# A chunked recurrence on one core: inverse levels as 32x32 products, a block last level, and a state sum on TensorE

## The chip, the cores and the metric

The kernel runs on one core of a Trainium2 chip, as one launch. The metric is the device time in microseconds (us), the median over runs. All products here are float32. In the profile such a product appears as two records (two weight loads and two matmuls), so "record" below means one of those two.

## The reference, cut to what matters

The program is a two-layer block network (layer 0: an RWKV-7 mixer and a SwiGLU; layer 1: a pooling mixer and a mixture of experts) followed by an attention layer. The change touches only the recurrence of the RWKV-7 mixer, which runs for 16 heads of width 64, in two directions, over 256 context and then 512 latent positions:

```python
def wkv7_scan(s0, r, w, kk, a, k, v):
    def step(s, inp):
        r_t, w_t, kk_t, a_t, k_t, v_t = inp
        s_kk = jnp.einsum('bhvk,bhk->bhv', s, kk_t)
        s = (s * w_t[:, :, None, :] - s_kk[..., None] * (kk_t * a_t)[:, :, None, :]
             + v_t[..., None] * k_t[:, :, None, :])
        return s, jnp.einsum('bhvk,bhk->bhv', s, r_t)
```

## The kernel before, in words

The function `pairs` does not step over positions. It cuts the 768 positions into 12 chunks of 64 (`CH`), numbered n; n = 0 to 3 are the context, n = 4 to 11 the latent part. Within a chunk the recurrence is a triangular system, and the kernel needs the inverse of a 64x64 triangular matrix. It works on 8 pairs of heads, p = 0 to 7. One head of the pair lies in partitions 0 to 63, the other in 64 to 127 (`heads`), and both directions (d = 0, 1) stand side by side in the columns. So each step handles four 64x64 matrices.

For each chunk the steps are, by their names in the plan:

- `score n` (L1168): products that give the matrix and the key products, masked by VectorE into `LK` (L1434). GpSimd adds the diagonal (`I`, L1056) and masks the first transposed inverse (`firstT`, L1059).
- `trans n` (L1184): PE transposes of the chunk's inputs by the identity, copied by ScalarE into `TR` (L1346).
- `first n` (L1438): VectorE's transpose of the first inverse.
- `X lev.n` and `T lev.n` for lev = 0 to 4: one doubling level of the inverse. X (L1192) is matrix times inverse, 4 products of 64x64; VectorE multiplies it by the level's mask into `Xs` (L1444). T (L1204) multiplies by the transposed inverse, again 4 products; ScalarE copies the new inverse into `TB` (L1350). VectorE's `turn lev.n` (L1441) transposes it for the next level.
- `akv n` (L1215, L1218), then the chain over chunks: `U n` (L1227, L1230; copy L1358), `Z n` (the state; L1237, L1239) and, for latent chunks, `Y n` (the output; L1252 to L1256, copy L1367). VectorE makes the new state from `Z n` in two steps: L1450 adds the old state to the product into `Z_sum`, L1455 multiplies by the decay into `Z`. `U n+1` waits for it.

The order is written out once as a list, `plan`, and every engine walks through it, each executing its own entries in order; semaphores (`Marks`) tie them together. Four chunks make a quad. `quad(g)` interleaves the front of quad g (score, trans, first, X, T, turn) with the chain of quad g-1: after each block of four X or four T entries one link of the chain stands (`U n`, or `Y n` and `Z n`), for the first eight blocks. `score` of the next quad waits until ScalarE has copied the last level of the chunk that held the same PSUM bank (L1350 from T4). The inputs of pair p+1 (`feature`: L1073 and L1099 on the PE; sigmoids, scans and reciprocals elsewhere) and the normalised outputs of pair p-1 (`output`) are spread over the quads by their place in the list. After the last pair one quad of chain alone remains. Input loads and masks are issued by SyncE's queue (L926 to L943).

Of the kernel before, what the change touches and what calls it, by code (L numbers as in the profile page):

```python
# [21 lines left out]
P = 128  # L22
# [403 lines left out]
class Kernel:  # L426
# [347 lines left out]
    def pairs(self, TW, TA, TG, YG, xr, s_wr):  # L774
# [5 lines left out]
        NG, LAST, H6, MASKS = N * QUADS, 4, TOK // 2, 12  # L780
        FRONT = ("score", "trans", "first", "X", "T", "turn")
# [24 lines left out]
        def quad(g):  # L806
# [61 lines left out]
        pe_f = self.marks("front_pe", [x for x in fronts if x.rstrip("0123456789.") in ("score", "trans", "X", "T")])  # L868
        pe_c = self.marks("chain_pe", links)
        act_f = self.marks("front_act", following(fronts, {"trans": ["tr"], "T": ["t"]}))  # L870
        act_c = self.marks("chain_act", following(links, {"akv": ["akv"], "U": ["U"], "Y": ["Y"]}))
        dve_f = self.marks("front_dve", following(fronts, {"score": ["LK"], "first": ["first"], "X": ["x"], "turn": ["turn"]}))
        dve_c = self.marks("chain_dve", [y for x in links if x[0] == "Z" for y in ([f"sum{x[1:]}"] if x != "Z0" else []) + [f"z{x[1:]}"]])
# [10 lines left out]
        with ExitStack() as st:  # L884
# [7 lines left out]
            Zb, Zs, Us = self.sb(st, "Z", 2, 2, CH), self.sb(st, "Z_sum", 2, CH), self.sb(st, "Us", 2, CH)  # L892
            mC, mL, mT = self.sb(st, "mask_score", 2, 4, CH), self.sb(st, "mask_level", 6, 2, CH), self.sb(st, "mask_turned", 2, CH)
            RB = self.sb(st, "r_rows", 4, SEQ)
            id2, scan = self.sb(st, "id_twice", CH), self.sb(st, "scan_steps", TOK)
            TB, AT, Xs = self.sb(st, "tb", 2, 4, 2, 2, CH), self.sb(st, "at", 4, 2, 2, CH), self.sb(st, "xs", 4, 2, CH)
# [3 lines left out]
            heads = (slice(0, CH), slice(CH, P))  # L900
            pair0 = COLS["pair"][0]
# [16 lines left out]
            with nc.Block() as block:  # L918
                @block.sync
                def _(sp):  # L920
# [17 lines left out]
                    for hh in heads:  # L938
# [3 lines left out]
                        sp.dma_start(mL[hh, :, :, :].rearrange("p l d n -> p (l d) n"), block("mL", hh, 12)).then_inc(s_mask, 16)  # L942
                        sp.dma_start(id2[hh, :], A["consts"][hh, hh]).then_inc(s_mask, 16)  # L943
                    r_load(0)
# [11 lines left out]
                def _(pool):  # L956
# [80 lines left out]
                    for kind, p, x in plan:  # L1037
# [13 lines left out]
                        if head == "score":  # L1051
                            if p == 0 and n == 0:
                                pool.wait_ge(s_diag, 2)
# [9 lines left out]
                def _(pe):  # L1063
# [56 lines left out]
                    for kind, p, x in plan:  # L1120
# [30 lines left out]

                        if head == "score":
# [32 lines left out]
                        elif head == "X":  # L1185
                            if lev:
# [3 lines left out]
                            for d in range(2):  # L1190
                                for hh in heads:
                                    last = pe.matmul(ps[hh, i, d * CH:(d + 1) * CH], M[hh, d, 0, :], tb[hh, d, 0, :],  # L1192
                                                     start=True, stop=True)
                        elif head == "T":
# [5 lines left out]
                            for d in range(2):  # L1200
                                to = 256 + d * CH
# [58 lines left out]
                def _(act):  # L1260
# [64 lines left out]
                    for kind, p, x in plan:  # L1325
# [22 lines left out]
                        elif head == "T":  # L1348
                            act.wait_ge(pe_f.sem, pe_f.at(x, p))
                            S.activation(TB[:, s, i, :, int(lev == LAST), :], ps[:, i, 256:384].rearrange("p (d n) -> p d n", d=2),  # L1350
# [20 lines left out]
                def _(dve):  # L1371
# [37 lines left out]
                    for kind, p, x in plan:  # L1409
# [13 lines left out]
                        if head == "score" and p == 0 and n == 0:  # L1423
                            dve.wait_ge(s_mask, MASKS * 16)
                            V.tensor_tensor(mL[:, :, :, :].rearrange("p l d n -> p (l d) n"), mL[:, :, :, :].rearrange("p l d n -> p (l d) n"),
                                            id2[:, :].unsqueeze(1).broadcast_to([P, 12, CH]), ALU.add).then_inc(s_diag, 1)
                            dve.wait_ge(s_diag, 1)
                            for d in range(2):
                                last = V.tensor_copy(mT[:, d, :], mL[:, 0, 1 - d, :])
                            last.then_inc(s_diag, 1)  # L1430
# [8 lines left out]
                        elif head == "turn":  # L1439
                            dve.wait_ge(act_f.sem, act_f.at(f"t{lev}.{n}", p))  # L1440
                            V.transpose(TB[:, s, i, :, 1, :], TB[:, s, i, :, 0, :]).then_inc(*dve_f.did(x))  # L1441
                        elif head == "X":
                            dve.wait_ge(pe_f.sem, pe_f.at(x, p))
                            V.tensor_tensor(Xs[:, i], ps[:, i, 0:P].rearrange("p (d n) -> p d n", d=2), mL[:, lev + 1, :, :],  # L1444
                                            ALU.mult).then_inc(*dve_f.did("x" + x[1:]))
                        elif head == "Z":
                            dve.wait_ge(pe_c.sem, pe_c.at(x, p))
                            b = ps[:, 5, 3 * P:4 * P].rearrange("p (d n) -> p d n", d=2)
                            if n:
# [1657 lines left out]
```

## Time and profile before

| what | value |
|---|---|
| median of 3 runs | 3277.22 us (3274.03 to 3282.49) |
| profiled execution, its own time | 3275.92 us |
| its span, first to last instruction | 3274.3 us |
| mean granted TensorE clock | 0.946 of full |
| PE, PEld busy | 2868.9 us, 2351.9 us |
| DVE, ACT, POOL busy | 1926.9 us, 1388.2 us, 536.5 us |

The recurrence runs from about 341 to 1132 us of the span. PE is TensorE's matmul, PEld its weight load, DVE VectorE, ACT ScalarE, POOL GpSimd, SPq SyncE's DMA issues. Matmuls are pipelined: a record lasts much longer than the distance to the next one's start, so the cost of one more record is read from distances of starts.

### The profile page before, as it was taken

Reading aid. Unit: us, or ns where it says so; the run is one execution under the profiler, and the core shown is the slowest. Engines: PE = TensorE matmul, PEld = TensorE weight load, DVE = VectorE, ACT = ScalarE, POOL = GpSimd, SP = SyncE. Lnnn points to the kernel's source line nnn. Section 1 sums busy time; section 2 is a strip of 40 time slices with the busy share of each in tenths; the row PEclk is TensorE's granted clock in tenths of the full one; section 3 lists DMA queues with packets and bytes.
Section 4 is the critical chain, followed back from the end, with each engine's and each line's share of the span. In section 5 each row is a group of like instructions: output and inputs, shape, how many; then the busy total and the mean of one; then the engine's idle time right before and its main releaser. Section 6 shows DMA issues by size and latency. Waiting matters only on the chain. (4 is left out here: it accounts for less than half of the span.)

```text
span 3274.3 us, 70012 instructions
## 1 busy us (share of the span) xinstructions
PE 2868.9 (88%) x30245; PEld 2351.9 (72%) x30245; DVE 1926.9 (59%) x3058; ACT 1388.2 (42%) x2040; POOL 536.5 (16%) x489
## 2 busy tenths in 40 slices
PE   7998798998989589999834999999976987779999
PEld 2564687787878467887614999999973754558877
DVE  5431455666565445765673888888876146456652
ACT  2002445445445333212223777777764335443331
POOL 3001445453344110000001000000010025200000
PEclk9999999999999789999966999999997989889999
DMA  5643000000000146664305999999962210122222
GB/s 194 221 154 103 7 20 20 20 21 20 10 14 4 64 152 242 264 266 162 124 13 227 372 370 364 369 366 365 371 256 68 94 52 26 52 80 102 90 101 79
DMA packets 74015, 483.10 MB, mean 148 GB/s; under 512 B 11123, under 2 KB 13043, under 8 KB 32288
## 3 DMA queue, kind: packets, MB, share of 16 engines
q1 hardware_dynamic: 59360, 418.48, 34.2%
q0 software_dynamic: 12096, 52.43, 4.4%
q10 hardware_dynamic: 2304, 8.39, 0.6%
q8 instruction: 208, 3.41, 0.4%
q14 instruction: 47, 0.39, 0.0%
HBM read 457.73 MB, written 34.13 MB: 150 GB/s over the span
## 5 line engine op out<-in xcount | busy, mean ns | idle before, releaser
L2267 DVE TENSOR_TENSOR sb_moe_w_lo<-w_ring,sb_moe_w_hi 128x1408 fp32r<-128x1408 f32 (+1 forms) x132 | 255.3, 1935 | 68.2 <-ACT sb_moe_w_hi L2221 67.3
L2167 PE MATMUL ps<-sb_moe_w_hi,sb_x_feat_lo 128*128 128x352 f32 x832 | 274.1, 329 | 11.5 <-DVE sb_moe_w_lo L2267 11.5
L2169 PE MATMUL ps<-sb_moe_w_hi,sb_x_feat_hi 128*128 128x352 f32 x832 | 268.4, 323 | 0.0
L2168 PE MATMUL ps<-sb_moe_w_lo,sb_x_feat_hi 128*128 128x352 f32 x832 | 267.6, 322 | 0.0
L2221 ACT ACTIVATE sb_moe_w_hi<-w_ring 128x2816 fp32r<-128x2816 f32 x80 | 204.4, 2556 | 0.2
L2167 PEld LDWEIGHTS ps<-sb_moe_w_hi,sb_x_feat_lo 128*128 128x128 f32 x832 | 156.8, 188 | 17.4 <-issue 17.0
L2167 PE MATMUL ps<-sb_moe_w_hi,sb_hid_feat_lo 128*128 128x256 f32 x572 | 163.2, 285 | 3.9 <-DVE sb_hid_feat_lo L2293 3.9
L2169 PE MATMUL ps<-sb_moe_w_hi,sb_hid_feat_hi 128*128 128x256 f32 x572 | 161.8, 283 | 0.0
L2168 PE MATMUL ps<-sb_moe_w_lo,sb_hid_feat_hi 128*128 128x256 f32 x572 | 161.8, 283 | 0.0
L1441 DVE STREAM_TRANSPOSE sb_tb<-sb_tb 128x128 f32<-128x128 f32 x384 | 106.0, 299 | 90.9 <-ACT sb_tb L1350 88.6
L2168 PEld LDWEIGHTS ps<-sb_moe_w_lo,sb_x_feat_hi 128*128 128x128 f32 x832 | 157.6, 189 | 0.0
L2169 PEld LDWEIGHTS ps<-sb_moe_w_hi,sb_x_feat_hi 128*128 128x128 f32 x832 | 156.7, 188 | 0.0
L1192 PEld LDWEIGHTS ps<-sb_tb,w_ring 64*64 64x64 f32 x3840 | 127.3, 135 | 38.5 <-issue 20.8
L1192 PE MATMUL ps<-sb_tb,w_ring 64*64 64x64 f32 x3840 | 145.4, 220 | 9.6 <-ACT sb_tb L1350 7.4
L233 PE MATMUL ps<-sb_ffn_features,sb_hi_ffn 128*128 128x512 f32 x352 | 141.2, 401 | 10.7 <-DVE sb_ffn_features L372 8.1
L233 PE MATMUL ps<-sb_conv_hl,sb_hi_conv 128*128 128x512 f32 x352 | 140.4, 399 | 10.2 <-DVE sb_conv_hl L372 10.2
L1434 DVE TENSOR_TENSOR w_ring<-ps,sb_mask_score 128x512 f32<-128x512 f32 (+1 forms) x96 | 57.8, 603 | 149.0 <-PE ps L1168 149.0
L1350 ACT ACTIVATE sb_tb<-ps 128x128 f32<-128x128 f32 x480 | 117.6, 279 | 63.3 <-PE ps L1204 59.8
L235 PE MATMUL ps<-sb_conv_hh,sb_hi_conv 128*128 128x512 f32 x352 | 140.6, 399 | 0.0
L234 PE MATMUL ps<-sb_conv_hh,sb_lo_conv 128*128 128x512 f32 x352 | 138.8, 394 | 0.0
L235 PE MATMUL ps<-sb_ffn_features,sb_hi_ffn 128*128 128x512 f32 x352 | 138.8, 394 | 0.0
L234 PE MATMUL ps<-sb_ffn_features,sb_lo_ffn 128*128 128x512 f32 x352 | 138.7, 394 | 0.0
(518 smaller groups left out, 7939.1 us busy)
## 6 DMA issues: line engine op xcount, KB each, us to landing
w_ring<-w_moe_up SPq DMA_DIRECT2D x67, 1408.0 KB, 8.4
sb_hm<-w_ada SPq DMA_DIRECT2D x48, 1024.0 KB, 6.9
w_ring<-w_ffn SPq DMA_DIRECT2D x22, 1024.0 KB, 4.8
w_ring<-w_up SPq DMA_DIRECT2D x22, 1024.0 KB, 4.9
sb_t_again<-w_moe_up SPq DMA_DIRECT2D x13, 1408.0 KB, 8.4
sb_hm<-w_moe_up SPq DMA_DIRECT2D x13, 1408.0 KB, 8.2
sb_b_again<-w_moe_up SPq DMA_DIRECT2D x13, 1408.0 KB, 7.6
w_ring<-w_moe_down SPq DMA_DIRECT2D x13, 1408.0 KB, 7.5
```

The costliest lines, as they stand in the source:

```text
L233: pe.matmul(out, w_hi[:, at:at + P], lo(k), start=(k == 0), stop=False)
L234: pe.matmul(out, w_lo[:, at:at + P], hi(k), start=False, stop=False)
L235: last = pe.matmul(out, w_hi[:, at:at + P], hi(k), start=False, stop=(k == KT - 1))
L1192: last = pe.matmul(ps[hh, i, d * CH:(d + 1) * CH], M[hh, d, 0, :], tb[hh, d, 0, :], start=True, stop=True)
L1350: S.activation(TB[:, s, i, :, int(lev == LAST), :], ps[:, i, 256:384].rearrange("p (d n) -> p d n", d=2), ACT.Copy).then_inc(*act_f.did("t ...
L1434: V.tensor_tensor(LK[:, s, i, :, ::by, :], ps[:, i, :].rearrange("p (d o n) -> p d o n", d=2, o=4)[:, :, ::by, :], mC[:, :, ::by, :], ALU. ...
L1441: V.transpose(TB[:, s, i, :, 1, :], TB[:, s, i, :, 0, :]).then_inc(*dve_f.did(x))
L2167: pe.matmul(out, x_lo, w_hi, start=first, stop=False)
L2168: pe.matmul(out, x_hi, w_lo, start=False, stop=False)
L2169: return pe.matmul(out, x_hi, w_hi, start=False, stop=end)
L2221: S.activation(WH[:, s, :], raw[r], ACT.Copy).then_inc(rounded[s], 1)
L2267: return V.tensor_tensor(WL[:, s, w], raw[raw_at(c, i)[0]][:, w], WH[:, s, w].bitcast(F32), ALU.subtract)
```

## The change

It has four parts.

1. Levels 0 to 3 (inverses of blocks up to 32 wide) no longer multiply whole 64x64 matrices but only their diagonal 32x32 blocks. Each head has two of them, so four 32-partition groups (`subs`) work side by side: X and T are each 8 products of 32x32 where there were 4 of 64x64. What VectorE masks, ScalarE copies and VectorE turns is 64 columns wide instead of 128. T of level 3 is written back to full width by VectorE (`wide3`, masked by `own_half`) instead of by ScalarE.
2. The last level is one 32x32 block off the diagonal per matrix: X4 is 4 products, T4 is 4, and a new entry `S4` (at the end of the quad) is 4 more; ScalarE copies after S4, and `score` of the next quad waits for that copy.
3. The old state is added in PSUM: `Z n` for n > 0 has 4 more 64x64 products with the identity, and VectorE's L1450 goes.
4. The level masks are loaded per 32-partition group: 22 mask DMAs instead of 12, and a few set-up instructions on VectorE.

```diff
-        NG, LAST, H6, MASKS = N * QUADS, 4, TOK // 2, 12
-        FRONT = ("score", "trans", "first", "X", "T", "turn")
+        NG, LAST, H6, MASKS, SUB = N * QUADS, 4, TOK // 2, 22, 32
+        FRONT = ("score", "trans", "first", "X", "T", "S", "turn")
...
+            out += [(p, f"S{LAST}.{n}") for n in cur]
...
+                    for g in subs:
+                        sp.dma_start(mL[g, :, :, :].rearrange("p l d n -> p (l d) n"),
+                                     block("mL", g, 2 * LAST + 2)[:, 2:2 * LAST + 2, :]).then_inc(s_mask, 16)
+                        sp.dma_start(id1[g, :], A["consts"][g, g]).then_inc(s_mask, 16)
...
+                        def across(d, g):
+                            own, to = subs[g], 256 + d * SUB
+                            pe.matmul(ps[subs[g ^ 1], i, to:to + SUB], x2[own, 0, :], tb[own, d, 1, homes[g]], start=True, stop=True)
+                            return pe.matmul(ps[own, i, to:to + SUB], tb[own, d, 0, homes[g]], ident[own, own], start=True, stop=True)
...
-                                for hh in heads:
-                                    last = pe.matmul(ps[hh, i, d * CH:(d + 1) * CH], M[hh, d, 0, :], tb[hh, d, 0, :],
-                                                     start=True, stop=True)
+                                for g in range(4):
+                                    cols = low if 0 < lev < LAST else homes[g]
+                                    if lev < LAST:
+                                        last = pe.matmul(ps[subs[g], i, d * SUB:(d + 1) * SUB], M[subs[g], d, 0, homes[g]],
+                                                         tb[subs[g], d, 0, cols], start=True, stop=True)
+                                    elif g % 2 == d:
+                                        last = pe.matmul(ps[subs[g ^ 1], i, 0:SUB], M[subs[g], d, 0, homes[g ^ 1]],
+                                                         tb[subs[g], d, 0, cols], start=True, stop=True)
...
-                                for hh in heads:
-                                    w, src = (tb[hh, d, 1, :], x2[hh, d, :]) if lev < LAST else (x2[hh, d, :], tb[hh, d, 1, :])
-                                    last = pe.matmul(ps[hh, i, to:to + CH], w, src, start=True, stop=True)
+                                for g in range(4):
+                                    own, cols = subs[g], low if 0 < lev < LAST else homes[g]
+                                    if lev < LAST:
+                                        last = pe.matmul(ps[own, i, to:to + SUB], tb[own, d, 1, cols], x2[own, d, :], start=True, stop=True)
+                                    elif d == 0 and g % 2:
+                                        last = across(d, g)
+                        elif head == "S":
+                            pe.wait_ge(pe_f.sem, pe_f.at("T" + x[1:], p))
+                            for g in (0, 2):
+                                last = across(1, g)
...
+                                if n:
+                                    for hh in heads:
+                                        pe.matmul(ps[hh, 5, to:to + CH], ident[hh, hh], Zb[hh, n % 2, d, :], start=False, stop=False)
...
+                        elif head == "T" and lev == LAST - 1:
+                            dve.wait_ge(pe_f.sem, pe_f.at(x, p))
+                            both, to = ps[:, i, 256:256 + CH], own_half[:, 0:2]
...
-                                V.tensor_tensor(Zs[:, :, :], b, Zb[:, n % 2, :, :], ALU.add).then_inc(*dve_c.did(f"sum{n}"))
```

## Rows read from the trace of the kernel before

**Rows 1.** The page: granted TensorE clock in 40 slices of the span.
```profile
PEclk9999999999999789999966999999997989889999
```
**Rows 2.** Busy time by stretch: start:end, length, each engine (xinstructions), clock, DMA.
```profile
341.00:380.00 39.00, 32.16 (x656) 25.38 (x658) 17.32 (x54) 15.55 (x34) 18.94 (x18) 0.87 0.01 2
380.00:1095.00 715.00, 648.45 (x18540) 584.33 (x18538) 432.89 (x1299) 348.38 (x954) 315.61 (x290) 1.00 0.05 15
1095.00:1132.00 37.00, 17.97 (x282) 13.10 (x278) 5.83 (x11) 6.40 (x18) 5.05 (x4) 0.64 0.00 1
```
**Rows 3.** Groups by line and shape: busy us, mean ns | idle before, and its releaser.
```profile
L1192 PE MATMUL ps<-sb_tb,w_ring 64*64 64x64 f32 x3840 | 145.4, 220 | 9.6 <-ACT sb_tb L1350 7.4 <-DVE sb_tb L1438 1.3
L1350 ACT ACTIVATE sb_tb<-ps 128x128 f32<-128x128 f32 x480 | 117.6, 279 | 63.3 <-PE ps L1204 59.8
L1204 PE MATMUL ps<-sb_xs,sb_tb 64*64 64x64 f32 x3072 | 114.7, 221 | 4.3 <-DVE sb_xs L1444 4.2
L1444 DVE TENSOR_TENSOR sb_xs<-ps,sb_mask_level 128x128 f32<-128x128 f32 x480 | 114.5, 272 | 26.4 <-PE ps L1192 26.4
L1441 DVE STREAM_TRANSPOSE sb_tb<-sb_tb 128x128 f32<-128x128 f32 x384 | 106.0, 299 | 90.9 <-ACT sb_tb L1350 88.6
...
L1346 ACT ACTIVATE w_ring<-ps 128x512 f32<-128x512 f32 x96 | 57.3, 597 | 66.5 <-PE ps L1184 66.5
...
L1434 DVE TENSOR_TENSOR w_ring<-ps,sb_mask_score 128x512 f32<-128x512 f32 x64 | 44.2, 691 | 83.7 <-PE ps L1168 83.7
...
L1450 DVE TENSOR_TENSOR sb_Z_sum<-ps,sb_Z 128x128 f32<-128x128 f32 x80 | 22.4, 280 | 51.6 <-PE ps L1239 51.5
```
**Rows 4.** PE in order of time, saturated: start us, us to the end, line, xrecords.
```profile
602.05 0.40 PE L1218 MATMUL ps<-sb_tb,w_ring 64*64 64x64 f32 x8
602.28 0.28 PE L1184 MATMUL ps<-sb_consts,sb_ex 64*64 64x64 f32 x4
```
**Rows 5.** PEld in order of time: weight loads of 128 columns for 2-column matmuls.
```profile
166.45 1.64 PEld L631 LDWEIGHTS ps<-sb_consts,sb_xx 128*128 128x128 f32 x14
```
**Rows 6.** Two lines' weight loads: duration ns min/median/max, first and last start, forms.
```profile
L631 PEld LDWEIGHTS ps<-sb_consts,sb_xx x64: 190/192/192, 166.1 to 237.0; 128*128 128x128 f32 x64
...
L2470 PEld LDWEIGHTS ps<-sb_hm,sb_head_sums x32: 106/110/110, 2617.0 to 2631.1; 128*32 128x32 f32 x32
```
**Rows 7.** PE and PEld in order of time, products 32 columns wide.
```profile
2616.96 1.92 PE L2470 MATMUL ps<-sb_hm,sb_head_sums 128*32 128x512 f32 x16
2618.81 0.50 PE L2453 MATMUL ps<-sb_lo_qkv,sb_qkv_hh 128*128 128x512 f32 x1
2616.96 0.16 PEld L2470 LDWEIGHTS ps<-sb_hm,sb_head_sums 128*32 128x32 f32 x8 [0.37 <-issue]
```
**Rows 8.** PE in order of time around feature products between X products.
```profile
637.44 0.68 PE L1192 MATMUL ps<-sb_tb,w_ring 64*64 64x64 f32 x16
638.05 1.56 PE L1073 MATMUL ps<-sb_tw,sb_w_pair 128*128 128x384 f32 x4
```
**Rows 9.** Waits inside the recurrence: engine line <- releaser, us in total, times, longest.
```profile
PE ps L1227 <- DVE sb_Z L1455: 35.7, 32, 2.7
PE ps L1073 <- ACT sb_sg L1275: 15.4, 8, 2.4
```
**Rows 10.** All engines in order of time, around one wait for the state.
```profile
586.11 1.10 PE L1192 MATMUL ps<-sb_tb,w_ring 64*64 64x64 f32 x32
586.68 0.91 DVE L1389 RECIPROCAL sb_kk<-sb_kk 128x128 f32<-128x128 f32 x1
587.51 0.23 DVE L1450 TENSOR_TENSOR sb_Z_sum<-ps,sb_Z 128x128 f32<-128x128 f32 x1
587.78 0.29 DVE L1455 TENSOR_TENSOR sb_Z<-sb_Z_sum,sb_pend 128x128 f32<-128x128 f32 x1
588.21 0.33 PE L1227 MATMUL ps<-sb_at,sb_tb 64*64 64x64 f32 x4 [1.00 <-DVE sb_Z L1455]
```
**Rows 11.** SyncE's queue: the last of the mask DMAs.
```profile
292.98 0.65 SPq L943 DMA_DIRECT2D sb_id_twice<-consts  x1
```

More of the change, by code:

```diff
@@ L866, in following @@
             return [y + x[len(x.rstrip("0123456789.")):] for x in names for y in table.get(x.rstrip("0123456789."), ())]
-        pe_f = self.marks("front_pe", [x for x in fronts if x.rstrip("0123456789.") in ("score", "trans", "X", "T")])
+        pe_f = self.marks("front_pe", [x for x in fronts if x.rstrip("0123456789.") in ("score", "trans", "X", "T", "S")])
         pe_c = self.marks("chain_pe", links)
-        act_f = self.marks("front_act", following(fronts, {"trans": ["tr"], "T": ["t"]}))
+        act_f = self.marks("front_act", following([x for x in fronts if not x.startswith((f"T{LAST - 1}.", f"T{LAST}."))],
+                                                    {"trans": ["tr"], "T": ["t"], "S": ["t"]}))
         act_c = self.marks("chain_act", following(links, {"akv": ["akv"], "U": ["U"], "Y": ["Y"]}))
-        dve_f = self.marks("front_dve", following(fronts, {"score": ["LK"], "first": ["first"], "X": ["x"], "turn": ["turn"]}))
-        dve_c = self.marks("chain_dve", [y for x in links if x[0] == "Z" for y in ([f"sum{x[1:]}"] if x != "Z0" else []) + [f"z{x[1:]}"]])
+        dve_f = self.marks("front_dve", [x for x in following(fronts, {"score": ["LK"], "first": ["first"], "X": ["x"], "turn": ["turn"],
+                                                               "T": ["wide"]})
+                                         if not x.startswith("wide") or x.startswith(f"wide{LAST - 1}.")])
+        dve_c = self.marks("chain_dve", [f"z{x[1:]}" for x in links if x[0] == "Z"])
         pool_f = self.marks("front_pool", following(fronts, {"score": ["I", "firstT"]}))
@@ L900, in pairs @@
             heads = (slice(0, CH), slice(CH, P))
+            subs = [slice(g * SUB, (g + 1) * SUB) for g in range(4)]
+            low, high = slice(0, SUB), slice(SUB, CH)
+            homes = (low, high, low, high)
             pair0 = COLS["pair"][0]
@@ L941, in _ @@
                                 sp.dma_start(mC[hh, d, o:o + 2, :], block("mK", hh, 4)[:, 2 * d:2 * d + 2, :]).then_inc(s_mask, 16)
[L942 removed]
+                        for d in range(2):
+                            sp.dma_start(mT[hh, d, :], block("mL", hh, 2)[:, 1 - d, :]).then_inc(s_mask, 16)
                         sp.dma_start(id2[hh, :], A["consts"][hh, hh]).then_inc(s_mask, 16)
+                    for g in subs:
+                        sp.dma_start(mL[g, :, :, :].rearrange("p l d n -> p (l d) n"),
+                                     block("mL", g, 2 * LAST + 2)[:, 2:2 * LAST + 2, :]).then_inc(s_mask, 16)
+                        sp.dma_start(id1[g, :], A["consts"][g, g]).then_inc(s_mask, 16)
                     r_load(0)
@@ L1185, in _ @@
                         elif head == "X":
-                            if lev:
+                            if lev == LAST:
+                                pe.wait_ge(dve_f.sem, dve_f.at(f"wide{lev - 1}.{n}", p))
+                            elif lev:
                                 pe.wait_ge(act_f.sem, act_f.at(f"t{lev - 1}.{n}", p))
@@ L1424, in _ @@
                             dve.wait_ge(s_mask, MASKS * 16)
+                            V.tensor_tensor(mT[:, :, :], mT[:, :, :], id2[:, :].unsqueeze(1).broadcast_to([P, 2, CH]),
+                                            ALU.add).then_inc(s_diag, 1)
                             V.tensor_tensor(mL[:, :, :, :].rearrange("p l d n -> p (l d) n"), mL[:, :, :, :].rearrange("p l d n -> p (l d) n"),
[L1426 to L1430, printed above, removed]
+                                            id1[:, :].unsqueeze(1).broadcast_to([P, 2 * LAST, SUB]), ALU.add).then_inc(s_diag, 1)
+                            for g in range(4):
+                                V.memset(own_half[subs[g], g % 2:g % 2 + 1], 1.0).then_inc(s_diag, 1)
+                                V.memset(own_half[subs[g], 1 - g % 2:2 - g % 2], 0.0).then_inc(s_diag, 1)
+                            dve.wait_ge(s_diag, 10)
                         if head == "score":
@@ L1439, in _ @@
                         elif head == "turn":
-                            dve.wait_ge(act_f.sem, act_f.at(f"t{lev}.{n}", p))
-                            V.transpose(TB[:, s, i, :, 1, :], TB[:, s, i, :, 0, :]).then_inc(*dve_f.did(x))
+                            cols = low
+                            if lev == LAST - 1:
+                                dve.wait_ge(dve_f.sem, dve_f.at(f"wide{lev}.{n}", p))
+                                cols = slice(0, CH)
+                            else:
+                                dve.wait_ge(act_f.sem, act_f.at(f"t{lev}.{n}", p))
```

41 lines of the change are left out of this document (25 added, 16 removed).

## The prediction

> **What bounds the kernel now.** I read the page first: the span is 3274.3 us and the TensorE clock is nearly always full [rows 1]. The chain that ended last lies wholly behind the recurrence, so it says nothing about the stage that is changed. The busy times by stretch do [rows 2]: in 380 to 1095 us TensorE is busy 648.5 of 715 us at clock 1.00, VectorE 432.9, ScalarE 348.4, GpSimd 315.6. So the recurrence is bound by TensorE with some 10% of waits in it. The next stage begins only when this block has ended, so what the recurrence saves comes off the end one for one.
>
> The groups by line [rows 3] say what TensorE does there: X (L1192) has 3840 records, T (L1204) as many, 3072 in the row shown and 768 of the last level. Their mean of 220 ns is not their cost, for they overlap. The cost is read in order of time [rows 4]: eight 64x64 records take 602.05 to 602.28; over many such pairs of rows it is 0.233 us, so 29.2 ns per record. The waits [rows 9] are led by U for the new state, 35.7 us in 32 times, and the second feature product for ScalarE's sigmoid, 15.4 us in 8.
>
> **Part 1, inverse as 32x32.** Per chunk X and T are now 5 levels x 2 x 4 products x 2 records = 80 records; over 96 chunks 7680 x 29.2 ns = 224.3 us. Changed, levels 0 to 3 are 4 x 2 x 8 x 2 = 128 records, X4, T4 and S4 8 each, 152 in all: 14,592 over 96 chunks. Everything hangs on what one costs.
>
> Two products of 64x64 on the two heads run together: a round of two records takes 58.3 ns. A single-file series of 128-column weight loads [rows 5] takes 1.64 us for fourteen, the last one's length counted in; less its 0.19 us [rows 6] that is 13 distances of 0.112 us. 58.3 and 112 ns lie on one line: 0.83 ns per weight column plus 5 ns. For 32 columns it gives 31.7 ns per round. How many records share a round? In [rows 7] four products, 32 columns wide with 512 moving ones, stand side by side: 16 records go by in 1.86 us, 0.116 us each, where 512 moving columns at the same 0.83 ns are 0.43 us; so four tiles do work at once. A record would then cost 31.7 / 4 = 7.9 ns.
>
> The bounds: from below, the eight weight loads of [rows 7] take 0.16 us with the last one's 0.11 us [rows 6] in it, so they start 7 ns apart, which is the fastest supply of records that I see: 6.7 ns x 14,592 = 98 us. From above, no row shows records at a lasting pace under 29.2 ns: 426 us. I take 7.9 ns: 115.3 us, a change of -109.0 us, for both the sharing and the weight line are in rows; but that TensorE is fed a pair of instructions every 8 ns for long stretches is in no row.
>
> Here a page speaks against the change. The row shows records starting 7 ns apart in a burst of eight. The Trainium skill (TensorE: Matmul & The Clock Gate, "Back-to-back issue gap"; TensorEngine Tiling, "Instruction Overhead") says that a matmul of fewer than about 60 columns costs as much as one of 60, about 25 ns from start to start. If that holds for each record, X, T and S cost 14,592 x 25 ns = 365 us, 141 us more than now; if it holds per tile, a round of 31.7 ns is above it and nothing changes. The burst speaks for the second, and proves it only for a burst. By the Trainium skill's 25 ns per record the kernel would take 3276 + 141 + 50 = 3467 us.
>
> **Changes of tile shape.** Feature products (128x128) between X products [rows 8]: sixteen records from 637.44 should be over at 637.91, the next form starts at 638.05. So 0.10 to 0.14 us are lost, and the other way it is similar: the four feature records take until 639.54, 1.49 us, where 4 x 0.323 = 1.29 are due. The next form's first record starts 0.07 us before the modelled end of the last one (637.44 + 0.68), and 0.20 us of the 1.49 are lost over two changes and a weight load of 128 columns. Walking through the plan, TensorE now changes form 130 times; with X, T and S at 32x32 between score, akv, trans, U, Y, Z at 64x64 it is 527 times. 397 more x 0.10 us = +39.7 us; bounds 0 (no loss between these two forms, which the trace doesn't have) and 0.17 us each, 67 us. The Trainium skill (TensorEngine Tiling, "Key Properties") has the rule that a change of tiling mode drains the engine; the trace agrees for the forms it has.
>
> **Part 2, the last level.** Before, X4 and T4 of a quad take 2 x 0.93 us, and each covers the other's hand-over. Hand-over times: a matmul ends 0.22 us after its start at 64 columns, so (less 32 x 0.83 ns) about 0.19 at 32; then about 0.06 us to the next engine, an estimate between 0.04 and 0.14, the distances behind L1450 and L1455 in [rows 10]; then VectorE or ScalarE. These cost 0.27 and 0.28 us at 128 columns; from 512 columns (0.69, 0.60) the slope is 1.1 and 0.8 ns per column, so 0.20 and 0.23 us at 64 [rows 3]. After, X4 is 4 x 8 x 7.9 = 0.25 us long, but T4.0 can start only 0.06 + 0.19 + 0.06 + 0.17 + 0.06 = 0.54 us after X4.0: 0.29 us idle. S4 is 0.25 us long, but the next quad's score waits for the copy behind S4.0, 0.06 + 0.19 + 0.06 + 0.23 + 0.06 = 0.60: 0.35 us. 24 quads x 0.64 = +15.4 us. In levels 0 to 3 the hand-over of about 0.6 us lies under a block of 0.51 us and the link behind it (0.47 to 1.4 us), but for the first quad and the odd late wait: +3 us. If no link covered it, it would cost 0.1 us per block, 192 blocks, 19 us.
>
> **Part 3, the state.** Ten of the twelve chunks of a pair get 4 products more: 80 x 8 x 29.2 ns = +18.7 us; both bounds are near, for it is the form of [rows 4]. L1450 goes from between Z and U. Where U waits [rows 9], X ends issuing at 587.05 and U starts at 588.21: VectorE had a reciprocal of 0.91 us in hand, then sum and scale. After: T's block is 0.42 us shorter and so is X's, the sum's 0.28 us are gone, identity and changes of form add 0.4; U is ready some 0.3 us earlier and the state some 0.7 us earlier. What is late next is the reciprocal, which stays. So of 35.7 us [rows 9] I take 8 off; bounds 0 and -20. In the last quad, which is chain alone, sum and identity weigh the same: 0.
>
> **The rest.** The feature product waits for a sigmoid that starts behind U's copy, a fixed time, so less TensorE work before it lengthens the wait by 0.2 us, 8 times: +1.6 us. VectorE's and ScalarE's shorter operations are off the path, hidden by TensorE's work: 0; were they the bound, it would be a gain. Level 3's copy moves to VectorE, 0.28 us at full width, in a stretch where it has 40% to spare. Mask loads: ten more DMAs at 0.65 us on SyncE's queue [rows 11] end at about 303 us, the masks are wanted at 344; behind them stand only the loads for r and pair 1, with tens of us of slack: 0. Without that slack it would be 6.5 us.
>
> **Sum.** -109.0 + 39.7 + 15.4 + 3.0 + 18.7 - 8.0 + 1.6 = -38.6 us. Against the profiled execution's own 3275.9 us that is 3237; it lies 1.3 us under the median of the runs, so 3238. The break-even is close: with the other terms as they are, the change pays only while a 32x32 record costs less than (224.3 - 70.4) / 14,592 = 10.5 ns.
>
> **Rivals.**
> *TensorE can't take small records that fast.* The supply of instructions, two per record, becomes the bound of each X and T block. For it: the trace has 14.6 ns per instruction as its best lasting pace. Against it: the bursts, and that the 64-column pace is explained by weight columns alone. It turns the sign from 10.5 ns per record. At 14.6 ns, half of today's distance, X, T and S cost 213 us (-11.3), the short-block stalls vanish, and with 39.7 + 18.7 - 8.0 the kernel takes 3316. At 29.2 ns, it is 3277 + 252 = 3529. I take 3316 as this rival's time. Chance 0.27.
> *Saved time comes back as waits.* Blocks of 0.5 us no longer cover the hand-over through VectorE and ScalarE, whose queues also hold reciprocals of 0.9 us. For it: [rows 9, 10], U already waits behind them. Against it: VectorE is busy only 61% of the stretch and its own work shrinks. If each of the 192 blocks in levels 0 to 3 idles 0.2 us more, it eats the 38 us: 3277. Chance 0.13.
> *No loss between 64x64 and 32x32.* Then -78 us: 3199. For it: the trace shows the loss only against forms with 128 rows. Against it: the loss stands on both sides of the feature products. Chance 0.10.
> *The clock falls.* Four 32x32 tiles work with a quarter of the array, two of 64x64 with half, and fewer records stand in a block. In 1095 to 1132 us, with TensorE busy under half, the granted clock averaged 0.64, between the levels of 1.2 and 2.4 GHz [rows 2]. If a quarter of the recurrence ran at the low level: 0.25 x 650 = 160 us more, about 3400. Against it: busy shares near 90% hold 1.00. Chance 0.05.
>
> **How the numbers follow.** My forecast, 3238, has 0.45. What a measurement of this kernel can tell from no change is 0.3%, 10 us. Faster: forecast, free change of form and a third of the waits rival, 0.59. Same: the rest of that rival, 0.09. Slower: the first rival and the clock, 0.32. The range for 8 in 10 reaches from the free change of form, 3195, to just past the first rival's 3316: 3325. The forecast's own range is 3215 to 3262.
>
> **What would show it.** Eight X products of a chunk (16 records) should follow one another in 0.13 us instead of the 0.23 us of eight records; by the first rival in 0.23 us or more. At each U, Y, Z between X and T a gap of 0.10 us or more. TensorE's busy time in the recurrence should fall by some 60 us. Between X4 and T4, and between S4 and score, idle of about 0.3 us each. The wait of U for the state should be below 35.7 us. I am wrong if X's records stand 12 ns or more apart, or if VectorE becomes the releaser of most T blocks.

## The result: 3.6% slower, and the profile after

The changed kernel takes 3392.95 us (3389.14 to 3398.11, 4 runs); the kernel before, beside it, 3275.62. The ratio is 1.036 (1.034 to 1.038): 117 us slower, where 39 us faster was forecast and 3325 us was the end of the range.

The page after, its span, the clock in 40 slices, and the packets, MB and time of the queue that brings instructions (before: 70012 instructions in a span of 3274.3 us, 208 packets; the clock in [rows 1]):

```profile
span 3392.8 us, 85054 instructions
PEclk8999898888988869999986799999997998889999
q8 instruction: 267, 4.37, 0.5%
```

Slices 4 to 14, counted from 0, are the recurrence, and only there does the clock differ much from [rows 1]. The busy times by stretch, for [rows 2]:

```profile
341.00:380.00 39.00, 30.04 (x900) 22.87 (x902) 15.59 (x57) 12.70 (x29) 20.00 (x18) 0.81 0.01 3
380.00:1100.00 720.00, 620.94 (x21935) 532.85 (x21934) 309.09 (x1123) 277.05 (x749) 284.45 (x259) 0.88 0.05 16
1100.00:1240.00 140.00, 114.32 (x4202) 101.52 (x4195) 45.91 (x195) 38.55 (x128) 30.00 (x34) 0.87 0.02 4
```

No engine is fuller than before. TensorE is busy 86% of the main stretch where it was 91%, VectorE 43% where it was 61%, and the clock is 0.88 instead of 1.00. So something keeps TensorE from its work that is none of the engines. The groups by line, for [rows 3] (L1214 is X, L1230 is T, L1389 and L1493 their copies, L1272 the identity products):

```profile
L1230 PE MATMUL ps<-sb_xs,sb_tb 32*32 32x32 f32 x6144 | 95.8, 201 | 28.6 <-issue 27.4 <-DVE sb_tb L1487 0.5 <-DVE sb_xs L1493 0.2
L1214 PE MATMUL ps<-sb_tb,w_ring 32*32 32x32 f32 x6144 | 89.6, 201 | 35.7 <-issue 31.7 <-DVE sb_tb L1479 3.4 <-ACT sb_tb L1389 0.5
L1389 ACT ACTIVATE sb_tb<-ps 128x64 f32<-128x64 f32 x384 | 69.5, 226 | 108.0 <-PE ps L1230 57.2 <-PE ps L1168 49.2
L1493 DVE TENSOR_TENSOR sb_xs<-ps,sb_mask_level 128x64 f32<-128x64 f32 x384 | 68.8, 209 | 57.7 <-PE ps L1214 55.9
L1272 PE MATMUL ps<-sb_Z,sb_consts 64*64 64x64 f32 x640 | 54.0, 245 | 1.6 <-issue 1.5
```

Read what ended the idle time before X and T: "issue", 31.7 and 27.4 us, meaning that no semaphore ended it. The list of waits, for [rows 9], shows each such stop to be long (total, times, longest):

```profile
PE ps L1214 <- issue: 31.7, 27, 3.1
PE ps L1230 <- issue: 27.4, 26, 2.7
PE ps L1086 <- ACT sb_sg L1310: 15.9, 7, 2.4
```

U's wait for the state, 35.7 us in 32 times before, has left the head of the list:

```profile
PE ps L1259 <- DVE sb_Z L1506: 1.5, 3, 0.5
```

In order of time TensorE looks like this (start, us to the end, records, idle before):

```profile
656.04 0.82 PE L1230 MATMUL ps<-sb_xs,sb_tb 32*32 32x32 f32 x64
656.79 0.33 PE L1287 MATMUL ps<-sb_FR,sb_Z 64*64 64x64 f32 x4
...
658.99 0.33 PE L1272 MATMUL ps<-sb_Z,sb_consts 64*64 64x64 f32 x4 [0.82 <-issue]
...
660.69 0.57 PE L1230 MATMUL ps<-sb_xs,sb_tb 32*32 32x32 f32 x38
662.47 0.42 PE L1230 MATMUL ps<-sb_xs,sb_tb 32*32 32x32 f32 x19 [1.22 <-issue]
```

The first line is a block of T as forecast: 64 records in 0.75 us to the next line's start, 11.7 ns each with the change of form. The last two are one block of T, broken after 38 of its 64 records by 1.22 us in which nothing is waited for (the view's window ends inside the last row; 26 records follow). I listed all stops over 0.45 us without a semaphore from 380 to 1215 us and counted TensorE's instructions between them: there are 91, 107.8 us in all, and each lies a whole multiple of 256 instructions behind the one before (256, 512, 768, give or take one). A record is two instructions, its weight load and its matmul, so the smallest distance is 128 records. Each stop ends 1.2 to 1.7 us after a 16 KB packet on the instruction queue has landed. In the kernel before there is one such stop, of 0.6 us.

To see where the 117 us lie I took TensorE's records from the recurrence's first to its last 64x64 product and split every distance between starts: array work (each record at its undisturbed pace: 29.2 ns, 7.9 ns, or the feature products' own); what the low clock level adds to it; up to 0.1 us (0.2 at the low level) at each change of form; gaps over 150 ns, with a semaphore ("waits") or without ("supply"); the rest, which is small idles. us:

```
                      before  after  difference  forecast
array work             631.7  542.0      -89.7      -90.3
low clock level          6.7   45.3      +38.6          0
changes of form         12.5   57.3      +44.8      +39.7
small idles             21.8   78.8      +57.0       }
waits on semaphores     97.2   64.2      -33.0       } +12.0
supply                   1.3  106.9     +105.6          0
length                 771.2  894.4     +123.2      -38.6
```

The two profiled spans differ by 118.5 us, so some 5 us of the 123.2 come back outside the recurrence. TensorE's busy time in it rose from 698.6 to 765.3 us, though its array work fell: changes of form and the low clock count as busy.

### The profile page after: what moved, and what is told of

Same layout as the page of the kernel before. It is cut to its first block and busy times, and to the rows that moved or that the text cites. A ratio compares the mean times of both kernels' runs of the same rounds, so it can differ in the third digit from the quotient of the medians.

```text
span 3392.8 us, 85054 instructions
## 1 busy us (share of the span) xinstructions
PE 2939.4 (87%) x37797; PEld 2387.6 (70%) x37797; DVE 1845.5 (54%) x3081; ACT 1346.8 (40%) x1944; POOL 533.2 (16%) x489
## 5 line engine op out<-in xcount | busy, mean ns | idle before, releaser
L233 PE MATMUL ps<-sb_ffn_features,sb_hi_ffn 128*128 128x512 f32 x352 | 141.2, 401 | 10.7 <-DVE sb_ffn_features L372 8.1
L1487 DVE STREAM_TRANSPOSE sb_tb<-sb_tb 128x64 f32<-128x64 f32 (+1 forms) x384 | 89.0, 249 | 102.0 <-ACT sb_tb L1389 101.2
L1713 DVE SCALAR_TENSOR_TENSOR sb_ada_acc<-sb_hm,sb_c_silu,sb_ada_acc 128x512 f32<-128x512 f32 x168 | 126.3, 752 | 10.5 <-DMA sb_hm<-w_ada 3.2
L1230 PE MATMUL ps<-sb_xs,sb_tb 32*32 32x32 f32 x6144 | 95.8, 201 | 28.6 <-issue 27.4
L1214 PE MATMUL ps<-sb_tb,w_ring 32*32 32x32 f32 x6144 | 89.6, 201 | 35.7 <-issue 31.7
```

Of the source, the lines that this page charges most:

```text
L233: pe.matmul(out, w_hi[:, at:at + P], lo(k), start=(k == 0), stop=False)
L1214: last = pe.matmul(ps[subs[g], i, d * SUB:(d + 1) * SUB], M[subs[g], d, 0, homes[g]], tb[subs[g], d, 0, cols], start=True, stop=True)
L1230: last = pe.matmul(ps[own, i, to:to + SUB], tb[own, d, 1, cols], x2[own, d, :], start=True, stop=True)
L1487: V.transpose(TB[:, s, i, :, 1, cols], TB[:, s, i, :, 0, cols]).then_inc(*dve_f.did(x))
L1713: V.scalar_tensor_tensor(out=ACC[:, j % 2, :], in0=w, scalar=scale, in1=ACC[:, j % 2, :], op0=ALU.mult, op1=ALU.add).then_inc(s_ada, 1)
```

## The experiments

The theory after the result: the instructions reach TensorE at a lasting pace of about 128 records per 3.5 us, records of 7.9 ns run through them faster, and the stops, the clock that falls with them, and the changes of form cost more than the array work saved. The rivals: the last level's uncovered hand-overs, or the new state sum, are what costs; or TensorE has a least distance per small record, wherever its instructions come from.

### Part 3 alone (e1_sum)

```diff
+                                if n:
+                                    for hh in heads:
+                                        pe.matmul(ps[hh, 5, to:to + CH], ident[hh, hh], Zb[hh, n % 2, d, :], start=False, stop=False)
...
-                                V.tensor_tensor(Zs[:, :, :], b, Zb[:, n % 2, :, :], ALU.add).then_inc(*dve_c.did(f"sum{n}"))
```

> The kernel before with part 3 alone: the old state is added by identity products on TensorE, VectorE's sum is gone. 1280 more records in the 64x64 form. Supply theory (TensorE gets its instructions in blocks of 256, no faster than one block per about 3.5 us, which is 13.7 ns per instruction; a 64x64 record already takes 14.6 ns per instruction, so this form stays just inside the supply): +18.7 us of TensorE work, less some of U's waits, 3280 to 3294, no stalls without a semaphore. Change-of-form theory (the slowdown comes from the 397 more changes between 64x64 and 32x32): the same, since no form changes here. If part 3 were the cause of the slowdown, 3340 or more.

Measured: 3257.84 us (3252.32 to 3265.81), ratio 0.994 (0.992 to 0.996): 20.7 us faster, faster than both kernels, and below what was expected. U's wait for the state falls from 35.7 us in 32 times to

```profile
PE ps L1227 <- DVE sb_Z L1454: 6.3, 15, 0.5
```

The identity products cost their 18.7 us (array work 650.3 against 631.7), and waits of all kinds fall by 40. The sum on TensorE is not what costs. But the stops without a semaphore, of which none was expected, are there: a dozen over 0.45 us, and supply rises from 1.3 to 12.9 us. So 64x64 records run into the supply too.

Why the wait fell so far is to be read from VectorE's operation that makes the new state, and from GpSimd beside it. Before (durations in ns as min/median/max, then the rows in order of time), and last the same operation in e1_sum:

```profile
L1455 DVE TENSOR_TENSOR sb_Z<-sb_Z_sum,sb_pend x80: 291/293/3161, 393.6 to 1112.5; 128x128 f32<-128x128 f32 x80
611.83 3.42 POOL L992 TENSOR_TENSOR sb_ex<-sb_ex,sb_kk 128x1536 f32<-128x1536 f32 x1
612.24 3.16 DVE L1455 TENSOR_TENSOR sb_Z<-sb_Z_sum,sb_pend 128x128 f32<-128x128 f32 x1
615.55 0.33 PE L1227 MATMUL ps<-sb_at,sb_tb 64*64 64x64 f32 x4 [1.55 <-DVE sb_Z L1455]
L1454 DVE TENSOR_TENSOR sb_Z<-ps,sb_pend x88: 226/291/293, 392.2 to 1103.7; 128x128 f32<-128x128 f32 x88
```

With the sum on VectorE, L1455 reads both its inputs from SBUF (`Z_sum` and `pend`). In 23 of 80 times it lasts 0.77 to 3.16 us instead of 0.29, and each of these ends 0.15 us after a GpSimd operation does; none of the short ones lies inside a long GpSimd operation. In e1_sum it reads PSUM and `pend`, and lasts 0.29 us at most in all 88, 33 of which lie inside a long GpSimd operation. Of U's 35.7 us, 21.6 in 17 times stood behind such a held L1455. The other 15 waits, behind the reciprocals and in the last quad, fell from 14.0 to 6.3 us.

### Everything but part 3 (e2_inverse)

The changed kernel with L1450's sum back on VectorE (the lines above the other way round).

> The changed kernel with part 3 taken back: parts 1, 2 and 4 alone. Both theories: most of the slowdown stays, 3370 to 3388, with some 90 stalls at block ends. It falls by more than the 18.7 us of identity products only if these fed the stalls: supply theory says a little more (10 blocks less at 3.5 us are 35 us at most, so 3358 at the lowest), change-of-form theory says exactly 19 us or less.

Measured: 3401.22 us, ratio 1.039 (1.036 to 1.041), above the range that both theories gave. Only 8 us are left of part 3's gain: U's wait for the state is 19.4 us here and 1.5 in the changed kernel, no more than the identity products cost. Supply costs 81 us and the low clock 56. The loss is in the inverse.

### The changed kernel with few small records (e3_few)

In X and T of levels 1 to 3 one 32x32 product is left where there are eight. This leaves out part of the inverse's work, while blocks, copies and semaphores stay.

```diff
-                                    if lev < LAST:
+                                    if lev < LAST and (lev == 0 or d + g == 0):
```

> The changed kernel, in which X and T of levels 1 to 3 issue one 32x32 product instead of eight (the other blocks of PSUM keep level 0's values, so the inverse is not computed). All waits, hand-overs, copies and all 527 changes of form stay; TensorE's records fall from 152 to 68 per chunk. Supply theory: the stalls at block ends vanish (under 10 us in all), the granted clock in the recurrence returns to 0.98 or more, and the time falls by well over the 84 x 96 x 7.9 ns = 64 us of array work, to 3200 to 3250, under the kernel before. Change-of-form theory: only the 64 us go, 3329.

Measured: 3259.43 us, ratio 0.994 (0.992 to 0.996). 8064 records fewer take away 134 us. At 7.9 ns they are 64 us of array work; supply falls from 106.9 to 18.1 (11 stops are left), the low clock from 45 to 34, and waits rise by 30. So the stops come with the number of instructions. The supply theory had expected more: under 10 us of stops, the clock at 0.98 or more and 3250 us or less. The same run says why it fell short: 172 us less array work than e1_sum (478.1 against 650.3), and the same time. Between those two stand changes of form (55.5 against 12.6), small idles (84.2 against 20.9), waits (93.7 against 57.1) and the clock (33.7 against 6.2).

### Part 2 alone, at 64x64 elsewhere (e4_last), and with part 3 (e6_last_sum)

```diff
+                                if lev == LAST:
+                                    for g in (d, d + 2):
+                                        last = pe.matmul(ps[subs[g ^ 1], i, 0:SUB], M[subs[g], d, 0, homes[g ^ 1]],
+                                                         tb[subs[g], d, 0, homes[g]], start=True, stop=True)
+                                    continue
...
+            out += [(p, f"S{LAST}.{n}") for n in cur]
```

> The kernel before with part 2 alone: levels 0 to 3 stay 64x64 products, the last level is one 32x32 block off the diagonal, with S at the end of the quad. 88 records per chunk instead of 80, of which 24 small; 48 more changes of form. By array work 96 x (467 - 190) ns = -26.6 us, +15.4 for the two uncovered hand-overs, +5 for changes of form: 3269. Supply theory: the 192 small instructions of a chunk-quad of X4, T4, S4 run ahead of the supply and wait at about one block end per quad for up to 1 us: 3272 to 3290. Change-of-form theory: 3265 to 3275.

Measured: 3324.93 us, ratio 1.015 (1.013 to 1.018): 46 us slower. U's wait for the state grew:

```profile
PE ps L1248 <- DVE sb_Z L1483: 45.1, 23, 2.7
PE ps L1159 <- DVE sb_xs L1470: 8.0, 15, 1.3
PE ps L1178 <- ACT sb_tb L1375: 4.5, 13, 1.0
```

Both theories had it well under 3300. The entries S4 lengthen the plan, and what is spread over it by place comes to stand elsewhere. Three times per pair U now waits long for the state: once 1.71 us behind a reciprocal (602.73 us), and twice, 2.7 and 2.2 us (622.37 and 635.18), behind the operation that makes the state, held while GpSimd works, as in e1_sum's rows. These held ones are 32.2 us of the 45.1. The other two rows are the last level's hand-overs. With part 3, where that operation reads PSUM, this can be told apart.

> Parts 2 and 3 without part 1: e4_last with the old state added on TensorE. In e4_last the largest wait is U for the state, 45 us, because the four S entries per quad shift the reciprocals' places in the plan onto the state's. If that is what made e4_last slow, taking VectorE's sum away removes some 25 to 30 us of it at +18.7 us of TensorE work, as it did in e1_sum: 3305 or a little less, still above the kernel before. If the uncovered hand-overs behind X4 and S4 are the cause, the waits of T4 and score stay and the time is the same 3305, with the state's wait under 15 us. If the two effects are independent, e4_last and e1_sum add up: 3278.5 + 46.4 - 20.7 = 3304.

Measured: 3278.26 us, ratio 1.000 (0.999 to 1.001), 20 us more than e1_sum, and 27 less than the 3305 expected: the two effects don't add up, for part 3 takes the held operations away. Its wait for the state:

```profile
PE ps L1248 <- DVE sb_Z L1482: 8.3, 9, 1.1
```

So part 2 beside part 3 costs 20 us. Array work is 26.5 us less than in e1_sum; waits (+13.0), supply (+12.5), the clock (+9.3), small idles (+10.7) and form (+4.8) are more.

### Parts 1, 3 and 4 with the last level at 64x64 (e8_levels)

```diff
-                                    elif g % 2 == d:
-                                        last = pe.matmul(ps[subs[g ^ 1], i, 0:SUB], M[subs[g], d, 0, homes[g ^ 1]],
-                                                         tb[subs[g], d, 0, cols], start=True, stop=True)
+                                    elif g < 2:
+                                        hh = heads[g]
+                                        last = pe.matmul(ps[hh, i, d * CH:(d + 1) * CH], M[hh, d, 0, :], tb[hh, d, 0, :],
+                                                         start=True, stop=True)
```

> Parts 1, 3 and 4 without part 2: levels 0 to 3 as 32x32 products, the last level again as four 64x64 products for X and for T, full-width mask and copy, no S. 144 records per chunk, 128 of them small. Supply theory: part 1 alone makes most of the slowdown, because its bursts of small records empty the instruction buffer: 3355 to 3385, with more than 60 stops at block ends. Last-level theory (the slowdown is the sum of what parts 1 and 2 do to the waits, and part 2 alone costs 46 us): 3393 - 46 = 3347 or less, with stops unchanged.

Measured: 3369.41 us, ratio 1.029 (1.027 to 1.031), 112 us more than e1_sum. With part 2's 20 us that makes 132 of the 135 us that lie between e1_sum and the changed kernel: on top of part 3 the other two add up. The stops are there (X, T, and the identity products in Z):

```profile
PE ps L1210 <- issue: 36.4, 36, 3.0
PE ps L1227 <- issue: 18.6, 19, 1.9
PE ps L1266 <- issue: 8.2, 4, 3.6
```

The last row has 64x64 products behind its stops, so a stop isn't tied to the small form: it comes wherever the 256th instruction stands.

### The same few records, at 64x64 (e7_few64)

e1_sum with one 64x64 product in X and T of levels 1 to 3 where there are four; leaves out the same work as e3_few.

```diff
-                                for hh in heads:
+                                for hh in heads[:2 if lev in (0, LAST) else 1]:
```

> e1_sum in which X and T of levels 1 to 3 issue one 64x64 product instead of four (the other blocks keep level 0's values, so the inverse is not computed). The counterpart of e3_few in the 64x64 form: 44 records per chunk at 29.2 ns are 1.28 us of array work, where e3_few has 68 at 7.9 ns, 0.54 us; but only 128 changes of form instead of 527. Hand-over theory (with blocks this short the way through VectorE and ScalarE bounds the levels, whatever the form): as e3_few, 3245 to 3265. Change-of-form theory (e3_few lost its gain to drains at each change and to the slower start after them): 3190 to 3225, clearly under e3_few although it has more array work.

Measured: 3224.18 us, ratio 0.985 (0.983 to 0.986). It has 71 us more array work than e3_few and is 35 us faster. The main stretch of both, e3_few first (PE, PEld, DVE, ACT, POOL, clock, DMA, GB/s):

```profile
380.00:1090.00 710.00, 639.72 (x18016) 546.93 (x18011) 338.67 (x1313) 301.48 (x863) 316.42 (x288) 0.91 0.05 15
```

```profile
380.00:1090.00 710.00, 637.00 (x16078) 564.99 (x16074) 386.45 (x1236) 345.39 (x976) 318.24 (x292) 0.95 0.06 19
```

Both are busy alike: a change of form and the modelled end of a record hide inside PE's busy time. Against its 71 us less array work e3_few has 43 us more in changes of form, 21 in small idles, 14 in waits, 18 by the clock and 18 in supply; that makes 43 us, where the medians of the runs differ by 35.

### TensorE alone (e5_bench)

A kernel of products alone, operands resident: 768 products of 64x64; 1024 of 32x32; 32 turns of 4 at 64x64 and 8 at 32x32; and 64 products of 32x32 in a hardware loop of 16 turns. It computes nothing of the reference.

```diff
+                    for j in range(1024):
+                        small(j)
...
+                    with pe.Fori(0, 16) as i:
+                        for j in range(64):
+                            small(j)
```

> TensorE alone, no other work and no waits between products; the output is a copy of the input. Sections with 128x128 products between them: (A) 768 products 64x64, (B) 1024 products 32x32 on four tiles, (C) 32 times four 64x64 and eight 32x32 products, (D) a loop of 16 turns over 64 products 32x32. Supply theory: A runs at 29.2 ns per record with few stalls; B starts at 7.9 ns per record, then 16.7 ns, and lastingly at 27 ns or more with a stop at every 256th instruction, 1024 x 2 x 27 = 55 us in all; C costs 48 instructions x 13.7 = 0.66 us per turn or more. Array theory (a small product costs what the array needs): B takes 1024 x 15.8 = 16 us, C 0.47 + 0.13 us and two changes of 0.1, 0.45 us per turn. D tells whether a loop, whose instructions are near, is free of the stops.

Measured, in order of time:

```profile
39.11 45.02 PE L494 MATMUL ps<-sb_bench 64*64 64x64 f32 x1536
...
91.40 1.54 PE L498 MATMUL ps<-sb_bench 32*32 32x32 f32 x159
94.75 1.27 PE L498 MATMUL ps<-sb_bench 32*32 32x32 f32 x128 [1.82 <-issue]
98.48 1.93 PE L498 MATMUL ps<-sb_bench 32*32 32x32 f32 x128 [2.46 <-issue]
102.48 1.93 PE L498 MATMUL ps<-sb_bench 32*32 32x32 f32 x128 [2.08 <-issue]
...
158.53 0.45 PE L494 MATMUL ps<-sb_bench 64*64 64x64 f32 x8
158.91 0.33 PE L498 MATMUL ps<-sb_bench 32*32 32x32 f32 x16
159.17 0.45 PE L494 MATMUL ps<-sb_bench 64*64 64x64 f32 x8
```

and the four stretches (PE, PEld, POOL, clock, DMA, GB/s):

```profile
39.10:83.90 44.80, 44.80 (x1535) 44.79 (x1536) 0.00 (x0) 1.00 0.02 4
91.40:147.70 56.30, 29.17 (x2049) 27.28 (x2048) 0.00 (x0) 0.56 0.02 5
157.26:178.70 21.44, 20.82 (x769) 16.91 (x768) 0.00 (x0) 1.00 0.02 4
186.10:208.60 22.50, 20.56 (x2049) 18.87 (x2048) 0.00 (x0) 1.00 0.00 1
```

The first line is the 29.2 ns of [rows 4] without a stop. The small records come in packs of exactly 128, every 3.5 to 4.0 us: 56.3 us / 2048 = 27.5 ns each, as slow as records four times as large. In the loop the same 2048 records take 22.5 us, 11.0 ns each, with hardly any DMA traffic and the clock at 1.00: within a turn of 128 they stand 8.4 ns apart, and between two turns there are 0.31 to 0.35 us from start to start. The first turn is

```profile
186.12 1.29 PE L498 MATMUL ps<-sb_bench 32*32 32x32 f32 x128
```

This decides against a least distance per small record. In the mixed section, 64x64 to 32x32 is 0.38 us for 0.233 of array work, and the way back 0.26 for 0.127: 0.13 to 0.15 us per change of form. Is that supply in disguise? A turn of 0.635 us is less than the 0.66 that the supply theory had as its least, and all but three of the turns take exactly that. At 48 instructions each they use up a block in 3.39 us, while the instruction queue's packets start 3.6 to 4.2 us apart here, so a turn draws on what was there already, and only the three longer ones (by 0.2 to 0.64 us) waited.

## Why the prediction was wrong, by its own steps

**Failed: the price of a 32x32 record over long stretches (part 1).** The prediction took 7.9 ns for all 14,592 records and said that no row shows TensorE fed a pair of instructions every 8 ns for long. The 7.9 ns are right for the array: rounds of four start 31.7 ns apart in bursts, and array work fell by 89.7 us where -109.0 + 18.7 = -90.3 was forecast. What failed is taking that as the price of time. A block of 256 instructions arrives at best about every 3.5 us (in e5_bench 3.69 on average over fourteen blocks). Before, 256 instructions were 128 records of 29.2 ns, 3.73 us of work: the supply just kept up, and none of the rows shown before the prediction told how close it was. Records of 7.9 ns empty a block in 1.0 us, and neither the 64x64 stretches nor the waits between refill what they drain. e5_bench shows it alone, e3_few and e8_levels show it in the kernel; it is worth 105.6 us. The sign that the prediction had set for it, X's records 12 ns or more apart, looks at the array's pace inside a block and doesn't see the stops.

The first rival had this mechanism, from 10.5 ns per record on, and took 14.6 ns and 3316 us for it. Its number was too low. Its own evidence was 14.6 ns per instruction, which is 29.2 ns per record, and it was priced at 14.6 ns per record; the lasting pace is 27.5 ns. At the recurrence's mix of wide and small records that pace isn't paid for every small one, so 3529 us, its upper case, was not reached either. And it let the other terms stand, while the stops brought the clock down with them.

The stops lie at every 256th instruction and end behind a 16 KB packet of the instruction queue. The Trainium skill (Runtime: NRT & Kernel Launch, "Instruction fetch mechanics") says that each engine's instructions are refilled in 16 KiB blocks of 256 and calls the cost of crossing a block "mostly hidden". The block size agrees with the trace. "Mostly hidden" holds for the kernel before (1 stop) and not for this one (91), and there the measurement decides.

The Trainium skill's 25 ns from start to start (TensorE: Matmul & The Clock Gate, "Back-to-back issue gap"), taken per record, gave 3467 us in the prediction. 27.5 ns measured straight looks like its proof and isn't: in the loop, the same records stand 11.0 ns apart.

**Failed: the clock at no cost.** It stood as a rival at 0.05 with 160 us; it cost 38.6 us, with 216 us of the recurrence at the lower of the two levels against 25 before. The drops come with the stops and idles rather than with the form of the products: in e5_bench the same 32x32 records ran at 0.56 with stops and at 1.00 without. e3_few, with 11 stops, still spent 152 us at the low level, so stops are not all that brings it down; which of the other idles does isn't shown.

**Right: changes of form.** 397 more at 0.10 us were forecast as 39.7 us; 44.8 were found, with a count that ends at 0.1 us each (0.2 at the low level); undisturbed changes cost 0.11 to 0.12 us over the array work in the changed kernel, and 0.13 to 0.15 in e5_bench. That is half of the array work saved. e3_few and e7_few64 bear on it: with 71 us less array work and 11 stops, e3_few is still the slower one, and 43 us of changes of form are its largest extra. Its blocks are shorter than those of a correct inverse, so this is a sign and not the price.

**Too small: hand-overs.** The last level was put at +15.4 us and levels 0 to 3 at +3.0. Small idles rose by 57.0 us in the changed kernel. Part of that is small records that run slower for a while: after the stop that ends at 554.3 us, 32 of them stand about 17.7 ns apart, though after most stops they run near 7.9 ns at once. I can't split it further. The second rival (waits take the gain) is not borne out by the waits on semaphores, which fell by 33 us; whether small idles are hand-overs isn't shown. In e3_few, whose blocks are too short to cover the way through VectorE and ScalarE, they are 93.7 us against e1_sum's 57.1.

**Too small on the good side: the state.** Forecast: +18.7 us of products and 8 us less of U's wait. The products cost that; the wait fell by 29 us in e1_sum. The prediction had read one wait, behind a reciprocal, and for that kind its 8 us were right: 14.0 fell to 6.3. It left out the other 17, 21.6 us, which stood behind L1455 while GpSimd held it up; with its first input in PSUM this no longer happens. L1455's 80 times took 57.3 us in the old trace, 716 ns each for an operation of 0.29 us. The bound of -20 was too narrow.

**Not foreseen: the plan's places.** S4 lengthens the list, and work spread by place moves: in e4_last +46 us, where the prediction's terms for part 2 give 15.4 - 26.6 of array work + 4.8 for 48 changes of form = -6.4. The prediction costed S4's hand-over and not what its place in the list does: which GpSimd operation or reciprocal the new state falls behind.

**Right or without effect:** the feature wait (15.4 to 15.9 us), the mask loads (the recurrence's first product at 343.5 us before, 345.1 after, and 345.8 in e1_sum with the old loads), narrower copies on VectorE and ScalarE off the path (0.21 and 0.23 us each, as worked out).

**Open.** Why a block takes 3.5 us to arrive wasn't varied, only avoided by a loop. That GpSimd holds up VectorE's operation with two SBUF inputs is read from the times; no run moved the GpSimd work alone. How much of the low clock's 38.6 us belongs to the stops and how much to the other idles isn't settled. e3_few and e7_few64 leave out products, so they show what costs time, not what a correct inverse could reach.

## What to carry to other kernels

Before cutting products into smaller ones, count instructions, not only array time: in unrolled code TensorE got 256 instructions per 3.5 us at best, so a float32 product, four instructions, costs 55 ns however small it is, unless longer ones around it leave a reserve. By these runs, smaller tiles pay only if their number does not rise and each stretch of one form is long against 0.13 to 0.15 us per change. The part that helped, moving the state's addition into PSUM accumulation, took an operation off the chain and, what was worth more, left VectorE's last step on it with only one input in SBUF, so that GpSimd no longer held it up; that paid more than its array time. So look at an operation's longest duration and not only at its median before deciding what a chain waits for.

## What the hardware showed that I had not expected

Instruction delivery as a bound: stops of 0.5 to 3 us at exact multiples of 256 instructions, shown by the profile only as "issue"; 64x64 records at 29.2 ns (3.73 us per block) lie just above it, e1_sum with 3% more of them had a dozen stops, and 32x32 ones lie far below. A hardware loop of 128 records has no such stops, only 0.31 to 0.35 us between its turns. The clock went to 0.56 in a stretch that was busy half of the time with identical work that held 1.00 without the stops. And a stop is charged to whatever stands there, so a group's idle time "<-issue" may have nothing to do with the group. And GpSimd holds up VectorE: an operation of 128x128 with both inputs in SBUF took up to 3.16 us instead of 0.29, always until 0.15 us after GpSimd's own had ended; with one input in PSUM it was never held.
